# Order of work on VectorE and ScalarE in a four-layer forward pass: low parts, scans, a recurrent branch and level updates

## The reference

```python
def rglru_group(h, w_in, conv_w, conv_b, w_r, b_r, w_i, b_i, lam):     # layer 0
    u, gate, xq = jnp.split(h @ w_in, [D_LRU, 2 * D_LRU], axis=-1)
    u = causal_conv4(u, conv_w) + conv_b
    r, i = sigmoid(blockwise(u, w_r) + b_r), sigmoid(blockwise(u, w_i) + b_i)
    log_a = -8.0 * r * softplus(-lam)
    a, b = exp(log_a), sqrt(-expm1(2 * log_a)) * (i * u)
    hs = scan(h_t = a_t * h_(t-1) + b_t)
    return hs * gelu(gate), xq

def memory_group(xq, mem, g_mem, w_kv, q_gain, k_gain):                # layers 0 and 1
    k, v = jnp.split(rms_norm(mem, g_mem) @ w_kv, [512], axis=-1)
    q, k = rms_norm(heads(xq), q_gain), rms_norm(heads(k), k_gain)
    return softmax(q @ k.T / sqrt(128)) @ v

def fox_group(h, ...):                                                 # layer 1
    s = q @ k.T / 8 + c[q] - c[k]; s = where(causal, s, -1e30)
    return softmax(s) @ v

def hgrn2_mixer(q, f_logit, i, g, ...):                                # layers 2 and 3
    S = f_t * S + k_t * v_t;  o = q_t . S;  o = rms_norm(o) * silu(g)
```

## Time and profile before

| what | us |
|---|---|
| median of 3 runs | 1380.65 |
| the three runs | 1380.65, 1374.33, 1380.74 |
| the profiled execution | 1375.35 |
| its span in the trace | 1373.2 |
| TensorE busy in it | 1325.1 |
| VectorE busy | 869.7 |
| ScalarE busy | 716.4 |

### The profile page before, as it was taken

The page is one execution under the profiler, slowest core; times in us unless marked ns, Lnnn a source line. Parts: engine busy times, 40 slices in busy tenths (PEclk is TensorE's granted clock), DMA queues, the critical chain, the costliest instruction groups (busy, mean ns, idle before and its releaser), DMA issues.

```text
span 1373.2 us, 18739 instructions
## 1 busy us (share of the span) xinstructions
PE 1325.1 (96%) x7309; PEld 1129.4 (82%) x7309; DVE 869.7 (63%) x1154; ACT 716.4 (52%) x1176; POOL 120.9 (9%) x158
## 2 busy tenths in 40 slices
PE   6969999999999999999999999999999999999998
PEld 5857888887888888888988778888889787788887
DVE  4875665657545656666765666666577756666665
ACT  5654544546565545446544455555465444555553
POOL 2102000003201200002101020000021010100000
PEclk9999999999999999999999899999999999999999
DMA  9433656555423565555631146555556222565551
GB/s 365 161 123 123 236 179 199 170 184 200 153 93 105 190 210 184 196 168 188 206 122 62 47 156 197 184 187 192 162 185 229 79 78 62 167 187 188 190 188 47
DMA packets 62327, 224.43 MB, mean 163 GB/s; under 512 B 7192, under 2 KB 7328, under 8 KB 62240
## 3 DMA queue, kind: packets, MB, share of 16 engines
q1 hardware_dynamic: 59616, 214.23, 47.1%
q0 software_dynamic: 1904, 6.82, 1.5%
q10 hardware_dynamic: 720, 2.19, 0.4%
HBM read 222.16 MB, written 1.05 MB: 163 GB/s over the span
## 4 chain that ended last, share of the span: by engine, by line
PE 80%; DVE 10%; ACT 5%; issue 2%; POOL 2%; DMA 0%; ACTq 0%; POOLq 0%; DVEq 0%
PE ps L323 15%; PE ps L277 15%; PE ps L282 15%; PE ps L281 15%; PE ps L327 8%; PE ps L433 3%; DVE wlo L1532 3%; PE ps L330 2%; PE ps L491 2%; PE ps L468 2%; PE ps L797 2%; PE ps L329 1%; DVE xn L1571 1%; ACT scr L1037 1%; ACT xn L1020 1%
## 5 line engine op out<-in xcount | busy, mean ns | idle before, releaser
L1532 DVE TENSOR_TENSOR wlo<-raw,whi 128x1024 fp32r<-128x1024 f32 (+1 forms) x402 | 479.3, 1212 | 268.9 <-ACT whi L983 267.1
L983 ACT ACTIVATE whi<-raw 128x1024 fp32r<-128x1024 f32 (+1 forms) x409 | 424.0, 1048 | 287.2 <-PE ps L323 178.6
L323 PE MATMUL ps<-XT,whi 128*128 128x512 f32 x896 | 318.6, 399 | 0.0
L327 PE MATMUL ps<-XT,wlo 128*128 128x256 f32 x896 | 251.5, 281 | 0.0
L323 PEld LDWEIGHTS ps<-XT,whi 128*128 128x128 f32 x896 | 168.4, 188 | 41.1
L277 PE MATMUL ps<-whi,HT_hi 128*128 128x512 f32 (+1 forms) x496 | 187.5, 378 | 1.6 <-DVE wlo L1532 1.0
L282 PE MATMUL ps<-whi,HT_lo 128*128 128x512 f32 (+1 forms) x496 | 186.3, 376 | 0.0
L281 PE MATMUL ps<-wlo,HT_hi 128*128 128x512 f32 (+1 forms) x496 | 186.2, 375 | 0.0
L327 PEld LDWEIGHTS ps<-XT,wlo 128*128 128x128 f32 x896 | 169.3, 189 | 1.2
L277 PE MATMUL ps<-whi,XT 128*128 128x512 f32 (+1 forms) x304 | 122.4, 403 | 7.6 <-DVE wlo L1532 5.3
L281 PE MATMUL ps<-wlo,XT 128*128 128x512 f32 (+1 forms) x304 | 118.0, 388 | 0.0
(11 more groups left out here) (253 smaller groups left out, 1837.8 us busy)
## 6 DMA issues: line engine op xcount, KB each, us to landing
raw<-in_w_m SPq DMA_DIRECT2D x152, 512.0 KB, 4.1
raw<-in_w_n SPq DMA_DIRECT2D x108, 512.0 KB, 4.2
raw<-in_w_c SPq DMA_DIRECT2D x48, 512.0 KB, 4.3
raw<-in_w_o SPq DMA_DIRECT2D x32, 512.0 KB, 3.6
raw<-in_w_kv SPq DMA_DIRECT2D x16, 512.0 KB, 4.6
raw<-in_w_b SPq DMA_DIRECT2D x16, 512.0 KB, 3.3
raw<-in_w_w SPq DMA_DIRECT2D x16, 512.0 KB, 4.8
raw<-in_w_a SPq DMA_DIRECT2D x12, 512.0 KB, 8.8
```

What stands on the lines that cost most here:

```text
L323: m = pe.matmul(outs[f][:, :], hi[:, j, at], both, start=(k == 0), stop=False)
L327: pe.matmul(outs[f][:, 0:T], lo[:, j, at], XT[0][:, k, :], start=False, stop=False)
L983: act.activation(whi[:, g % NSPLIT, 0:w], raw[:, g % NRAW, 0:w], ACT.Copy).then_inc(split_hi, 1)
L1532: dve.tensor_tensor(wlo[:, g % NSPLIT, 0:w], raw[:, g % NRAW, 0:w], whi[:, g % NSPLIT, 0:w].bitcast(F32), ALU.subtract).then_inc(split_lo, 1)
```

## The change

The same arithmetic is done by the same instructions, but for one small extra exponential; PE's matmuls stay in their order. What moves:

1. Layer 0, DVE: `log1p` and its followers stand ahead of `fox_sums(1)` and of `norm_lo(1, 0)`, with the low parts in it.
2. Layer 0, DVE: the four scans alternate with low parts (`splits` of one more unit ahead of the second and the third scan).
3. Layer 0, DVE: `fox_sums(2)` stands ahead of the low part of unit 18, and the low part of unit 19 behind the gelu.
4. Layer 0, ACT: a 128x4 exponential behind the square root, with the load of its table there; the load ahead of the first softmax falls away.
5. Layer 0: the recurrent branch's split (`MX_hi` on ACT, `rglru_lo` on DVE) and all low parts up to unit 22 stand ahead of the first maximum; the gains (`second_gains`) move behind the second. PE's first scores no longer wait until the memory values are copied; the copies move behind the first exponentials.
6. `soft`: the first maximum of each attention has up to four more units' low parts ahead of it. In layer 1 this moves three.
7. Layer 1, DVE: the low part of the first key unit stands between `norm_rows(4, 0)` and `norm_rows(4, 1)`.
8. Layers 2 and 3, DVE: `advance(2)` ahead of `ch_silu(1)`, `advance(4)` ahead of `branch(1, 0)`, `hgrn_rows` ahead of `cmp_add`.

```diff
@@ PE @@
-            mem_ready(0)
+            mem_ready(0, 2)
...
-            attend(["ma0"], {"ma0": mem_spec(0)}, {(2, 2): lambda: (pe.wait_ge(ev("ylo"), 1), next(out_left)),
+            attend(["ma0"], {"ma0": mem_spec(0)}, {1: lambda: mem_ready(0), (2, 2): lambda: (pe.wait_ge(ev("ylo"), 1), next(out_left)),
@@ ACT @@
             act.activation(slot(8, 1024), slot(8, 1024), ACT.Sqrt, scale=-0.25).then_inc(ev("bsq"), 1)
+
+            act.activation(sm("z4", 4), sm("z4", 4), ACT.Exp)
+            splits(fills["mk0.0"].pos + 2)
...
-            for tt in range(TT):
-                copy_out(f"mv0.{tt}", slot(6, 1024)[:, tt * BLK:(tt + 1) * BLK])
-
-            def rglru_hi():
-                act.wait_ge(ev("yrow"), 1)
-                act.activation(MX[0][:, 0:4, :].rearrange("p f t -> p (f t)"), slot(4, 1024), ACT.Copy).then_inc(ev("yhi"), 1)
-
-            soft(["ma0"], {1: rglru_hi})
+            splits(fills["mv0.1"].pos + AHEAD)
+            f = fills["mv0.1"]
+            act.wait_ge(bank_full[f.bank], f.turn)
+            act.wait_ge(ev("yrow"), 1)
+            act.activation(MX[0][:, 0:4, :].rearrange("p f t -> p (f t)"), slot(4, 1024), ACT.Copy).then_inc(ev("yhi"), 1)
+
+            def mem_values_in():
+                for tt in range(TT):
+                    copy_out(f"mv0.{tt}", slot(6, 1024)[:, tt * BLK:(tt + 1) * BLK])
+
+            soft(["ma0"], {0: mem_values_in})
@@ DVE @@
-                    ps = full(f"{tag}.s{i}", 0)
+                    ps = full(f"{tag}.s{i}", 0 if n else NSPLIT)
...
             gain_column(sm("mgcol", 2)[:, 0:1], P, rg("xaq0"), rg("xak0"))
-            fox_sums(1, sm("cq", 16)[:, 0:8], hq(8, P).rearrange("p n d -> p (n d)"), P)
-            norm_lo(1, 0, MX)
             dve.wait_ge(ev("lamexp"), 1)
             log1p(l4, z, w4, t4)
...
             dve.tensor_scalar(sm("hb", 8)[:, 0:8], cg("br", 0, 8), 0.5, None, ALU.mult).then_inc(ev("lru_c"), 1)
+            fox_sums(1, sm("cq", 16)[:, 0:8], hq(8, P).rearrange("p n d -> p (n d)"), P)
+            norm_lo(1, 0, MX)
             norm_lo(1, 1, MX)
...
             for f in range(4):
+                if f < 3:
+                    splits(fills["mk0.0"].pos + f)
                 step(dve.tensor_tensor_scan(om[:, f * T:(f + 1) * T], decay[:, f * T:(f + 1) * T],
...
+            fox_sums(2, sm("rk8", 8), hq(8, P).rearrange("p n d -> p (n d)"), P)
             splits(fills["mk0.1"].pos + AHEAD)
-            fox_sums(2, sm("rk8", 8), hq(8, P).rearrange("p n d -> p (n d)"), P)
-            splits(fills["mv0.0"].pos)
...
             gelu()
-
-            fg = sm("fgcol", 1)
-            gain_column(sm("mgcol", 2)[:, 1:2], P, rg("xaq1"), rg("xak1"))
-            gain_column(fg, 64, rg("foxq"), rg("foxk"))
-            dve.memset(fg[64:65, :], 1.0).then_inc(ev("gcols"), 1)
-            soft(["ma0"], {1: rglru_lo, 3: lambda: rows_out(["ma0"], "ma0", 0, xn[:, 0, 512:1024])})
+            splits(fills["mv0.1"].pos + AHEAD)
+            rglru_lo()
+            soft(["ma0"], {1: second_gains, 3: lambda: rows_out(["ma0"], "ma0", 0, xn[:, 0, 512:1024])})
...
-            for tt in range(TT):
-                norm_rows(4, tt, slot(8 + tt, 1024))
+            norm_rows(4, 0, slot(8, 1024))
+            splits(fills["q.1"].pos + 1)
+            norm_rows(4, 1, slot(9, 1024))
...
-                            2: lambda: (ch_silu(1), advance(2)),
-                            3: lambda: (advance(3), branch(1, 0), advance(4), cmp_values()),
+                            2: lambda: (advance(2), ch_silu(1)),
+                            3: lambda: (advance(3), advance(4), branch(1, 0), cmp_values()),
...
-                            11: lambda: (gates(), cmp_add(0), cmp_add(1), hgrn_rows())})
+                            11: lambda: (gates(), hgrn_rows(), cmp_add(0), cmp_add(1))})
```

5 lines of the change are left out of this document (added).

## The result

The changed kernel takes 1366.86 us, the median of 6 runs (1365.76 to 1371.27). The kernel before took 1379.97 beside it (6 runs, 1374.33 to 1381.60). The ratio is 0.9917, with a 95% interval of 0.9895 to 0.994. In two later comparisons, each on a chip of its own, the ratio was 0.994 [0.9921, 0.9958] and 0.9933 [0.9913, 0.9952]: 1368.24 against 1375.36, and 1367.12 against 1375.77. So the change is worth 7 to 13 us, and rather 8 or 9 than 13. The kernel before had medians of 1376.18, 1375.36, 1375.77 and 1377.18 in the four later comparisons, lower than the 1379.97 of the first.

The account below looks back on a forecast made before the run. TensorE was taken as the bound, busy 1325.1 of 1373.2 us, so reordering could win only its 48 us of idle time and its lowered-clock time. Terms summed to -10.9 us, from 1378.0 to 1367.1, range 1358 to 1376.

Parts of the forecast that it names:

- Unit 7: Layer 0: starts 3.5 us later behind 4.6 idle; a swallowed 1.71 wait for `norm_lo` leaves a net +1.8.
- Unit 19: Layer 0: its low part, now behind the scaled keys and the gelu, makes PE wait anew, net +3.4 us.
- Layer 1's wait: Layer 1's attention: the 2.00 us wait for a low part goes, plus 1.6 of clock, -3.6 us.
- the key unit: Layer 1: its low part moves between two norm halves, so the 0.71 us wait goes, -0.7 us.
- Rival A: Removed waits return as others in layers 1 to 3, and layer 0 loses another 1: 1373.3 us, 15 in 100.
- the levels: Layers 2 and 3: PE's waits of 1.53 and 0.51 us go, together -2.0 us in each layer.
- `hgrn_rows`: -1.3 and -0.8 predicted: Layers 2 and 3: moved ahead of `cmp_add`, it wins DVE's idle time before the output projection, -1.3 and -0.8 us.
- Layer 0: -0.5 predicted: Layer 0 to the attention's third turn: gains and losses net -0.5 us, one clock fall set against another.
- Layer 3: -2.8 predicted: Layer 3: -2.0 us from the level order and -0.8 from `hgrn_rows` ahead of `cmp_add`, no clock term.
- rival B: Clock helps more: fewer idle times bring fewer falls, another 5 us, 1362.1 us, 15 in 100.
- rival C: Slower than before, through clock falls from layer 0's idle times of 4.6 and 2.9 us: 1379.1 us, 3 in 100.
- Its own marks of failure: Wrong if idle falls under 6 us, layers 1 or 2 wait over 1 us for exponential or maximum, or over four fall places.

Follow-up runs that it names:

- e3_rows: The kernel before with only `hgrn_rows` moved ahead of `cmp_add` in layers 2 and 3: 1377.87 us against 1376.18, ratio 1.0012.
- e8_rows_apart: The changed kernel with the recurrent branch's two turns and the two additions interleaved on DVE: 1364.04 us, ratio 0.9906 to the kernel before.
- e4_layer0: The kernel before with all of the change's layer 0 edits and nothing else: 1374.73 us against 1376.18, ratio 0.9991.
- e7_no_log1p_early19: The changed kernel with the softplus group behind the first low part again and unit 19's low part made early again: 1364.45 us, ratio 0.9915 to the kernel before.
- e5_after_again: The changed kernel itself, run again beside its variants: 1368.24 us against 1375.36 for the kernel before, ratio 0.994.
- e11_after_third: The changed kernel itself, run a third time on another chip: 1367.12 us against 1375.77 for the kernel before, ratio 0.9933.
- e2_levels: The kernel before with only the level updates moved ahead of `ch_silu(1)` and `branch(1, 0)` in layers 2 and 3: 1370.12 us against 1376.18, ratio 0.9959.
- e6_no_log1p: The changed kernel with DVE's softplus group (`log1p`) behind layer 0's first low part again: 1364.50 us, ratio 0.9917 to the kernel before.
- e9_no_log1p_rows_apart: The changed kernel with the softplus group put back and the recurrent turns interleaved with the additions: 1364.84 us, ratio 0.9915 to the kernel before.
- e10_all: The changed kernel with softplus group and unit 19's low part put back, recurrent turns interleaved, early exponential removed: 1362.53 us, ratio 0.99 to the kernel before.

## Why the prediction was right, and where it was not

The measured time, 1366.86, is 0.2 from the 1367.1 predicted. That it is so near is luck, since several terms missed and their errors cancel; the terms say more than the sum.

**Right, with their size.** Unit 7 starts at 43.19 behind 4.62 of idle time (predicted: near 43.4, 4.6) and the wait for `norm_lo` is gone. From the turn behind `norm_lo` to unit 16 PE wins 1.65 (48.69 became 51.74, 76.49 became 77.89; predicted 1.75). Unit 19 loses 3.3 (85.53 became 90.25, so 4.7 late instead of 1.4; predicted 3.4). Layer 1's wait is gone with nothing in its place, and the first turn of probabilities has moved by 3.8 since the key unit (predicted 3.6). Rival A, that waits come back as others, did not happen in layer 1 or in the levels; it did in the recurrent branch's rows, where 1.77 became 0.32 and 1.81.

**The restart.** All waits were costed at their length. Each wait removed gave 0.24 to 0.3 us more: 1.0 for the key unit instead of 0.7, 2.5 for the levels instead of 2.0 in each layer. The mechanism was right, the terms were a little small.

**`hgrn_rows`: -1.3 and -0.8 predicted, 0.1 or less measured.** The step that failed is "so the gain is what DVE stood idle there". It followed the DVE work up to `rows_lo` and took for granted that PE's turns would come as early as their inputs. It left out that `cmp_add` does two things: it produces a sum, and it frees bank 7. In the old order the second of them was done in time and hidden; in the new one it is what PE waits for, 1.81 us. e3_rows shows the loss alone, e8_rows_apart its removal.

**Layer 0: -0.5 predicted, +0.4 in the pair of traces, and no difference in e4_layer0's time.** The waits are as computed. The step that failed set one fall of the clock against another, and it was wrong by one: the long wait of 4.62 brought one at 43 us, that of 2.60 at unit 19 one at 91, and only the one at 102 went. With them PE stands 1.4 us late at unit 16 (predicted 0.0), 4.7 at unit 19 (3.4), 6.2 at the attention's first turn (3.5) and 1.8 at the third (-0.5); only behind that does before pay its own fall. That the low part of unit 19 behind the gelu cost 3.4 "as the one new wait that I am sure of" was right for its place, and e7_no_log1p_early19 shows that most of it was no loss: the attention waits for DVE's low parts anyway.

**Layer 3: -2.8 predicted, +1.0 in the trace.** The edits act there as in layer 2 (up to level 7 the same 2.5, from 69.83 to 67.32 us), but the falls in the compression stretch and at the output projection cost 6.8 us in place of 1.7. From level 7 to the cut in the MLP it takes 86.34 us (1095.31 to 1181.65) where before took 82.81 (1105.30 to 1188.11): 3.5 more, which with the 2.5 won are the +1.0. The four traces of the changed order (after, e5_after_again, e8_rows_apart, e11_after_third) have 5.1 to 6.8 in layer 3, those of before 1.7 and 3.4. The prediction gave the clock no term here; it had it as a help in rival B and, as a loss, only in layer 0 (rival C). What decides the length of a fall there is open: e2_levels, with the level order alone, has 6.8 as well, and e6_no_log1p 5.1, but e7_no_log1p_early19, e9_no_log1p_rows_apart and e10_all, which differ from the changed kernel only in layer 0 and in the rows' order, have 3.4.

**Why the number came out all the same.** The gain was put at 10.9 us. Term by term the removed waits gave 9 to 10 (4.8 in layer 1 with its fall, 2.5 in each of layers 2 and 3, nothing in layer 0 and for the rows), about 1 in the mean came from falls behind the waits of 1.53, and some 2 to 4 were given back by longer falls in layer 3. Against its own neighbours the gain is 7 to 9 us in the two later comparisons and 13 in the first. The predicted time took 1378.0 as the kernel before, higher than all four later medians; so against the later comparisons a gain put some 2 us too high stood against a base some 2 us too high. In the first comparison it is the other way round: the kernel before took 1379.97, 2.0 more than assumed, and the gain was 13.1, 2.2 more. The best estimate of the gain over all three comparisons (their mean, 9.6) is smaller than the term sum. The longer falls in layer 3 belong to the pair of profiled executions and not to the kernels: the granted clock of that of before was 0.992, of that of the changed kernel 0.988, while over all executions for which it is on record the mean is 0.9894 for the kernel before (72) and 0.9896 for the changed one (16). Their mean times are 1376.4 and 1367.5. So on the whole the clock neither gave nor took, and the 8.9 us between them are near the 8.3 of the waits with their restarts (1.0 and 2.3 in layer 1, 2.5 in each of layers 2 and 3).

**Its own marks of failure.** PE's idle sum fell by 7.8, more than the 6 asked for, and no row of layers 1 or 2 waits over 1 us for an exponential or a maximum. But the falls stand in six places of the four layers, not in four at most: by this mark the prediction was wrong on the clock. The mark was a poor one: the kernel before has five itself. The prediction had not found the one at 1133, took the two at 761 and 781 (5.1 us) for one of some 3.4, and in rival C put a fall at 2.0 us where the row gives 4.00 x 0.43 = 1.7.

**The scatter.** Two executions of one kernel differ by up to 8.5 us (1372.4 to 1380.9, in 31 runs of before). The prediction supposed that the slower ones had more falls of the clock. The granted clock on record for each of the 31 bears this out: the sixteen with 0.991 or 0.992 took 1372.4 to 1376.4 us, the four with 0.986 took 1379.3 to 1380.9. The difference of 0.005 to 0.006 is 7 or 8 us at the lowered clock's cost, of which about 6 show in the time. Where such falls stand, no trace of so slow an execution tells; the two traces of before show that they move: the first has none behind the wait of 1.53, the second two, and one at 76 us, but none at 781. They cost 10.2 us in sum in one and 11.9 in the other. The same holds for a single order of work: the ten executions of e2_levels had a granted clock between 0.987 and 0.995 and took 1365.9 to 1375.6 us.

## What to carry to other kernels

When an instruction is moved behind another on its engine, write down everything it releases, buffers and banks too, not only the value it makes: `cmp_add` was put off as "not needed yet", and PE then waited 1.81 us for the bank that it read. A low part or a maximum that is late by 2 us costs more than 2 us, the restart each time and a fall of the clock often; so order work by who waits for it, but do not pay for it with one long wait, since here 4.6 us of idle time in one piece cost 3.0 and bought nothing. And take the order of falls from more than one trace: a gain of 2.5 us per layer up to level 7 stood in every trace but one, and could still vanish in one layer's total.
